# Start of a two-layer hybrid trunk: small first pieces of x, half of x's squares on GpSimd, warm-up products

## The reference

```
xn   = rms_norm(h, norm_g)                  # mean of squares over 2048
proj = xn @ w_in                            # 2048 x 5376
qa, fa, ia, ga, qb, kb, vb, gb, uc, gc = split(proj)
ya = rms_norm(hgrn2(qa, fa, ia))            # 4 heads of 128, gated linear recurrence
yb = window_attention(rope(norm(qb)), rope(norm(kb)), vb, sinks)   # 16 heads of 64, window 128
yc = pooled means (windows 2/4/8/16) minus the token, linear map, scale
h  = h + concat(ya*silu(ga), yb*silu(gb), yc*silu(gc)) @ w_out
```

## Time and profile before

| | us |
|---|---|
| median of three runs | 1633.53 |
| profiled execution: span from first to last instruction | 1632.0 |
| runs shown, above that span | 1.4 to 1.6 |
| PE busy | 1612.1 (99% of the span) |
| DVE busy | 915.2 (56%) |
| ACT busy | 645.5 (40%) |
| POOL busy | 20.8 (1%) |

### The profile page before, as it was taken

The page is one execution under the profiler, slowest core; times in us unless marked ns, Lnnn a source line. Parts: engine busy times, 40 slices in busy tenths (PEclk is TensorE's granted clock), DMA queues, the critical chain, the costliest instruction groups (busy, mean ns, idle before and its releaser), DMA issues.

```text
span 1632.0 us, 27854 instructions
## 1 busy us (share of the span) xinstructions
PE 1612.1 (99%) x11366; PEld 1493.0 (91%) x11366; DVE 915.2 (56%) x1897; ACT 645.5 (40%) x1280; POOL 20.8 (1%) x78
## 2 busy tenths in 40 slices
PE   6999999999999999999999999999999999999999
PEld 6999999999999999999998899889999988888887
DVE  7677877645666554434335678774555674443231
ACT  7676455423222432323237764553223233232121
POOL 0000000000000000000000000000000000000000
PEclk9999999999999999999999999999999999999999
DMA  6222210112121223344432221112111212234441
GB/s 251 79 104 78 79 53 29 51 53 78 57 74 62 94 80 115 124 138 135 140 118 79 103 78 66 39 52 78 53 68 63 79 52 103 104 121 137 145 147 48
DMA packets 28014, 147.23 MB, mean 90 GB/s; under 512 B 3568, under 2 KB 3696, under 8 KB 12656
## 3 DMA queue, kind: packets, MB, share of 16 engines
q1 hardware_dynamic: 27888, 145.46, 25.8%
HBM read 136.86 MB, written 8.52 MB: 89 GB/s over the span
## 4 chain that ended last, share of the span: by engine, by line
PE 96%; DVE 2%; issue 1%; ACT 0%; DMA 0%; SPq 0%; DVEq 0%
PE ps_gemm L816 80%; PE ps_mix L706 3%; PE ps_mix L742 3%; PE ps_mix L658 2%; PE ps_mix L672 2%; PE ps_mix L701 1%; PE ps_gemm L634 1%; DVE rstd L900 1%; PE ps_mix L786 1%; PE ps_mix L788 0%; PE ps_mix L718 0%; PE ps_mix L775 0%; PE ps_mix L737 0%; DVE w_lo L883 0%; DMA w_stage<-in_w_in 0%
## 5 line engine op out<-in xcount | busy, mean ns | idle before, releaser
L816 PE MATMUL ps_gemm<-x_hi,w_hi 128*128 128x264 f32 (+1 forms) x2304 | 561.7, 311 | 12.5 <-DVE w_lo L883 10.3
L816 PE MATMUL ps_gemm<-x_hi,w_lo 128*128 128x264 f32 (+1 forms) x2304 | 543.1, 304 | 0.0
L816 PE MATMUL ps_gemm<-x_lo,w_hi 128*128 128x264 f32 (+1 forms) x2304 | 542.6, 303 | 0.0
L816 PEld LDWEIGHTS ps_gemm<-x_hi,w_hi 128*128 128x128 f32 x2304 | 371.1, 189 | 32.9 <-DVE w_lo L883 11.1
L816 PEld LDWEIGHTS ps_gemm<-x_hi,w_lo 128*128 128x128 f32 x2304 | 370.8, 189 | 16.5
L816 PEld LDWEIGHTS ps_gemm<-x_lo,w_hi 128*128 128x128 f32 x2304 | 370.2, 189 | 14.4
L883 DVE TENSOR_TENSOR w_lo<-w_stage,w_hi 128x512 fp32r<-128x512 f32 x464 | 305.5, 689 | 104.0 <-ACT w_hi L440 92.7
L440 ACT ACTIVATE w_hi<-w_stage 128x512 fp32r<-128x512 f32 x464 | 265.3, 618 | 169.7 <-DVE z L960 122.7
L816 PE MATMUL ps_gemm<-mixed_hi,w_lo 128*128 128x264 f32 (+1 forms) x768 | 205.2, 322 | 0.0
L816 PE MATMUL ps_gemm<-mixed_lo,w_hi 128*128 128x264 f32 (+1 forms) x768 | 205.0, 321 | 0.0
L816 PE MATMUL ps_gemm<-mixed_hi,w_hi 128*128 128x264 f32 (+1 forms) x768 | 203.9, 320 | 0.0
(11 more groups left out here) (169 smaller groups left out, 1407.1 us busy)
## 6 DMA issues: line engine op xcount, KB each, us to landing
w_stage<-in_w_in SPq DMA_DIRECT2D x83, 1024.0 KB, 4.8
w_stage<-in_w_out SPq DMA_DIRECT2D x32, 1024.0 KB, 4.8
x_in<-in_xT SPq DMA_DIRECT2D x4, 1056.0 KB, 9.8
res<-in_xT SPq DMA_DIRECT2D x16, 264.0 KB, 3.0
h1T<-z SPq DMA_DIRECT2D x16, 264.0 KB, 3.4
res<-h1T SPq DMA_DIRECT2D x16, 264.0 KB, 3.0
out<-z SPq DMA_DIRECT2D x16, 256.0 KB, 3.2
rope<-in_c_rope SPq DMA_DIRECT2D x2, 528.0 KB, 3.6
```

The source lines that it names most:

```text
L816: ins = pe.matmul(g[:, bank, 0:size], ws[:, N % 2, tick], xs[:, k, c:c + size], start=tick == 0 and i == 0, stop=tick == TICKS - 1 and i == 2)
```

## The change

x comes in five pieces of 1, 3, 4, 4 and 4 tiles. prm and the first quarter of chunk 0's weights are issued from ScalarE's queue, not SP's. The squares of tiles 0 to 7 are made and added up by GpSimd into `vt`, as it gets the tiles (15 instructions, each waiting for the one before). Those of tiles 8 to 15 stay on ScalarE and VectorE, but leave the loop over k: they follow the weight quarters of chunk 1 at ticks 2, 5 and 8 (VectorE a tick later), four, two and two at a time. At tick 13 VectorE waits for GpSimd and adds `vt` to `rstd`. TensorE begins with three float32 matmuls of 512 columns on zeros, for which VectorE clears `z[:, 0]` whole.

```diff
+X_PIECES = ((0, 1), (1, 4), (4, 8), (8, 12), (12, 16))
+POOL_SQUARES = 8
+ACT_SQUARES = ((8, 9, 10, 11), (12, 13), (14, 15), ())
+SUMS_END = (KC - POOL_SQUARES + 1, 2 * KC - POOL_SQUARES + 1)
+WARM_MATMULS = 3
...
-            sp.dma_start(prm_sb[:], prm).then_inc(s_prm0, 16)
             load_x(0)
-            sp.dma_start(wst[:, 0, 0:4]..., w_in[0, 0, :, 0:4 * P]).then_inc(s_wfirst, 16)
             load_x(1)
+            load_x(2)
             sp.dma_start(wst[:, 0, 4:]..., w_in[0, 0, :, 4 * P:]).then_inc(s_w[0], 16)
-            load_x(2)
             load_x(3)
+            load_x(4)
             load_w(1)
...
                     sp.wait_ge(s_xlo, 16)
-                    sp.wait_ge(s_xsq, 16)
+                    sp.wait_ge(s_xsq, KC - POOL_SQUARES)
+                    sp.wait_ge(s_psq, 2 * POOL_SQUARES - 1)
...
+            for k in range(POOL_SQUARES):                       # GpSimd
+                for q, (k0, _) in enumerate(X_PIECES):
+                    if k == k0:
+                        pool.wait_ge(s_x[q], 16)
+                if k == 0:
+                    pool.tensor_tensor(vt[:], xin[:, 0], xin[:, 0], ALU.mult).then_inc(s_psq, 1)
+                else:
+                    pool.tensor_tensor(th[:], xin[:, k], xin[:, k], ALU.mult).then_inc(s_psq, 1)
+                    pool.wait_ge(s_psq, 2 * k)
+                    pool.tensor_tensor(vt[:], vt[:], th[:], ALU.add).then_inc(s_psq, 1)
+                    pool.wait_ge(s_psq, 2 * k + 1)
...
+            act.dma_start(prm_sb[:], prm).then_inc(s_prm0, 16)  # ScalarE
+            act.dma_start(wst[:, 0, 0:4]..., w_in[0, 0, :, 0:4 * P]).then_inc(s_wfirst, 16)
             act.wait_ge(s_prm0, 16)
...
                 x_high(0, k, xin[:, k])
-                if 1 <= k <= EARLY_SQUARES:
-                    x_square(0, k - 1, xin[:, k - 1])
...
-                    if N == 0 and tick == 12:
-                        for k in range(EARLY_SQUARES, KC):
+                    if N == 0 and tick in HI_TICKS:
+                        for k in ACT_SQUARES[HI_TICKS.index(tick)]:
                             x_square(0, k, xin[:, k])
...
+            pe.wait_ge(s_warm, 1)
+            for _ in range(WARM_MATMULS):
+                pe.matmul(M[:, 0], z[:, 0, 0:P], z[:, 0, 0:512], start=True, stop=True)
...
-            link(dve.memset(z[:, :, 0:PAD], 0.0))
+            link(dve.memset(z[:, 1, 0:PAD], 0.0))
+            dve.memset(z[:, 0, :], 0.0).then_inc(s_warm, 1)
...
-                if 1 <= k <= EARLY_SQUARES:
-                    x_sum(0, k - 1)
...
                     if N == 0 and tick == 13:
-                        for k in range(EARLY_SQUARES, KC):
-                            x_sum(0, k)
+                        dve.wait_ge(s_psq, 2 * POOL_SQUARES - 1)
+                        dve.wait_ge(s_ss, SUMS_END[0] - 1)
+                        dve.tensor_tensor(rstd[:], rstd[:], vt[:], ALU.add).then_inc(s_ss, 1)
...
                         w_low(N + 1, HI_TICKS.index(tick - 1))
+                        if N == 0:
+                            for k in ACT_SQUARES[HI_TICKS.index(tick - 1)]:
+                                x_sum(0, k)
```

More of the change, by code:

```diff
@@ L77, in mini_tick @@
     return RMS_TICK if MINI[n][0] == "rms" else MINI_TICK
-EARLY_SQUARES = 8
+X_PIECES = ((0, 1), (1, 4), (4, 8), (8, 12), (12, 16))
[3 more added lines that the diff above has]
+WARM_MATMULS = 3
 ROPE_CHUNKS = list(range(1, 10))
@@ L257, in build @@
         s_prm, s_prm0, s_rope = sem("const_in"), sem("prm_in"), sem("rope_in")
-        s_x = [sem(f"x_in{q}") for q in range(4)]
+        s_x = [sem(f"x_in{q}") for q in range(len(X_PIECES))]
+        s_warm, s_psq = sem("zeros_for_warm_up"), sem("pool_square_step")
         s_w = [sem("w_in0"), sem("w_in1")]
@@ L354, in load_x @@
             def load_x(q):
-                sp.dma_start(xin[:, 4 * q:4 * q + 4], xT[:, 4 * q:4 * q + 4]).then_inc(s_x[q], 16)
-            sp.dma_start(prm_sb[:], prm).then_inc(s_prm0, 16)
+                k0, k1 = X_PIECES[q]
+                sp.dma_start(xin[:, k0:k1], xT[:, k0:k1]).then_inc(s_x[q], 16)
             load_x(0)
-            sp.dma_start(wst[:, 0, 0:4].rearrange("p k c -> p (k c)"), w_in[0, 0, :, 0:4 * P]).then_inc(s_wfirst, 16)
             load_x(1)
+            load_x(2)
             sp.dma_start(wst[:, 0, 4:].rearrange("p k c -> p (k c)"), w_in[0, 0, :, 4 * P:]).then_inc(s_w[0], 16)
-            load_x(2)
             load_x(3)
+            load_x(4)
             load_w(1)
@@ L414, in _ @@
                     pool.wait_ge(s_xlo, 16)
-                    pool.wait_ge(s_xsq, 16)
+                    pool.wait_ge(s_xsq, KC - POOL_SQUARES)
                 pool.memset(vm[:], 0.0).then_inc(s_avz, 1)
@@ L448, in x_square @@
             def x_square(layer, k, src):
-                if 16 * layer + k >= 2:
-                    act.wait_ge(s_ss, 16 * layer + k - 1)
+                if layer:
+                    act.wait_ge(s_ss, SUMS_END[0] + k - 1)
+                elif k >= POOL_SQUARES + 2:
+                    act.wait_ge(s_ss, k - POOL_SQUARES - 1)
                 act.activation((ta_, tb_)[k % 2], src, ACT.Square).then_inc(s_xsq, 1)
+            act.dma_start(prm_sb[:], prm).then_inc(s_prm0, 16)
+            act.dma_start(wst[:, 0, 0:4].rearrange("p k c -> p (k c)"), w_in[0, 0, :, 0:4 * P]).then_inc(s_wfirst, 16)
             act.wait_ge(s_prm0, 16)
@@ L459, in _ @@
             for k in range(KC):
-                if k % 4 == 0:
-                    act.wait_ge(s_x[k // 4], 16)
+                for q, (k0, _) in enumerate(X_PIECES):
+                    if k == k0:
+                        act.wait_ge(s_x[q], 16)
                 x_high(0, k, xin[:, k])
-                if 1 <= k <= EARLY_SQUARES:
-                    x_square(0, k - 1, xin[:, k - 1])
                 if k % 4 == 0:
@@ L504, in _ @@
                         w_high(N + 1, HI_TICKS.index(tick))
-                    if N == 0 and tick == 12:
-                        for k in range(EARLY_SQUARES, KC):
+                    if N == 0 and tick in HI_TICKS:
+                        for k in ACT_SQUARES[HI_TICKS.index(tick)]:
                             x_square(0, k, xin[:, k])
                     if n == 1 and tick == RMS_TICK - 2:
-                        act.wait_ge(s_ss, 16 * layer + 16)
+                        act.wait_ge(s_ss, SUMS_END[layer])
                         act.activation(sqh[:], rstd[:], ACT.Copy).then_inc(s_sqh, 1)
@@ L894, in x_sum @@
                 sq = (ta_, tb_)[k % 2]
-                dve.wait_ge(s_xsq, 16 * layer + k + 1)
-                if k == 0:
+                first = 0 if layer else POOL_SQUARES
+                done = SUMS_END[0] if layer else 0
+                dve.wait_ge(s_xsq, layer * (KC - POOL_SQUARES) + k - first + 1)
+                if k == first:
                     dve.tensor_copy(rstd[:], sq).then_inc(s_ss, 1)
                 else:
-                    dve.wait_ge(s_ss, 16 * layer + k)
+                    dve.wait_ge(s_ss, done + k - first)
                     dve.tensor_tensor(rstd[:], rstd[:], sq, ALU.add).then_inc(s_ss, 1)
@@ L1204, in _ @@
                     if n == 1 and tick == RMS_TICK - 1:
-                        dve.wait_ge(s_ss, 16 * layer + 16)
+                        dve.wait_ge(s_ss, SUMS_END[layer])
                         square_low(norm_no(layer, n), sql[:], rstd[:], sqh[:])
```

## The result

The changed kernel takes 1641.4 us (median of 5 runs, 1641.25 to 1642.07), against 1633.53 for the kernel before: a ratio of 1.0048, 95% interval 1.0037 to 1.0059. It is 7.9 us slower. The profiled span is 1639.5 us, 7.5 above the 1632.0 of before.

The account below looks back on a forecast made before the run. PE bounds the kernel from 42 us, so only M's shift counts: first pieces and squares -3.2, turns with GpSimd +12.2, issues and warm-up 0, net +9.0, giving 1642.5 us; 8 in 10 range 1630 to 1651.

Parts of the forecast that it names:

- What bounds the kernel: From 42 us PE is busy; the whole change is a shift of M, the sum products, with N=2 4.32 us behind.
- Eight squares on GpSimd: Fifteen GpSimd instructions of 1.2 us take turns with VectorE's two-input ones before M: M +12.2 us.
- The 0.5 taken off for one-input instructions: On VectorE's chain before M: GpSimd reads beside semaphore gaps, copy, cast and first sum save 0.5 us in all.
- Rival 1: VectorE isn't held up by long GpSimd instructions: M 34.5, 3.2 us earlier, 1630.3 us; chance 0.22.
- rival 2: GpSimd keeps VectorE out for half its length only: M 39.4, 1.7 us later, 1635.2 us; chance 0.09.
- rival 3: GpSimd, over 1.7 us an instruction, is last by itself at vt's add: M 38.6, 1634.4 us; chance 0.04.
- First pieces: At the start, smaller x pieces bring the first product near 6.9, 2.3 us earlier; k=4 still waits for weights at 12.2.
- Two issues on ScalarE's queue: At the start, issues done by 1.7 us, before prm is used: 0 to +0.5 us on the first product, taken as 0.
- Squares out of the x loop: On VectorE in the x loop: x_lo ends at 22.2, 3.8 us earlier, chain behind 12.25; M 34.5, 3.2 earlier.
- Warm-up: Three products on zeros before PE's first product: at worst it comes 1.1 us late, k=4 has slack; taken as 0.
- a step of 0.12 from the start: Sign to look for in PE's first products: steps of 0.12 us, where 24 products had taken 0.22 each.
- Rival 4: Slow VectorE delivery drops PE to 0.22 a step; N=1 up to 2.8 us more, some 1 showing; within the 0.62 case.

Follow-up runs that it names:

- experiment 1: Changed kernel with GpSimd's fifteen instructions left out (squares of tiles 0 to 7 missing from the sum, add of vt replaced by an equal one): 1629.68 us.
- experiment 4: Changed kernel with four squares on GpSimd instead of eight, the other twelve late on ScalarE and VectorE: 1637.66 us.
- experiment 5: Changed kernel with no square on GpSimd, all sixteen made by ScalarE and added by VectorE behind the x loop: 1636.09 us.
- experiment 9: Whole computation, no GpSimd squares; unlike the kernel before, TensorE sums ScalarE's squares of tiles 0 to 7, sum product at tick 9, w's second quarter separate: 1629.66 us.
- experiment 2: Changed kernel with GpSimd's fifteen instructions turned into memsets of the same size, squares of tiles 0 to 7 not summed: 1629.4 us.
- experiment 7: Kernel before with the five x pieces only, all issues left on SP, w's first quarter ahead of the second x piece: 1634.66 us.
- experiment 6: Kernel before with only the five x pieces and the two issues on ScalarE's queue, squares and warm-up as before: 1634.1 us.
- experiment 8: Kernel before with only the three warm-up products on zeros added: 1634.5 us.

## Why the prediction was right

*What bounds the kernel.* Right. The change is a shift of the sum product M, and N=2 follows 4.3 us behind it: 4.31 after, 4.32 in experiment 1. It fails only where TensorE waits so long for M that its clock falls (6.1 in experiments 4 and 5), and where TensorE itself is the bound (4.8 in experiment 9).

*Eight squares on GpSimd*, the deciding step, forecast +12.2 on M. Measured +11.9, by leaving them out, with VectorE's step, GpSimd's rows and the end of the effect all as told. That the size came out so near is in part luck, because errors in it cancelled. An instruction takes 1.07, not 1.2, and a turn costs 0.93, not 1.1. Against that, I counted 2.8 us of idle VectorE between 7.4 and 12.9 (experiment 1 has 1.3 there), and let 3.5 of 15 turns fall into it and ahead of it for nothing, while 11.9/0.93 = 12.8 were paid, all but some 2. The 0.5 taken off for one-input instructions was not seen: GpSimd was done before those came. Rival 1 is refuted by the x_lo rows and experiment 1, rival 2 by the turn of 0.93 of 1.07, and rival 3 by GpSimd's end at 28.9, far ahead of the add of vt at 41.46.

The Trainium skill, SBUF - State Buffer (Who interferes with whom), has the order right: two inputs on VectorE against a reading GpSimd exclude each other, and a GpSimd that only writes does no harm (experiment 2 agrees, four x_lo in 2.81). Its "whole instruction" is slightly more than was measured, 0.93 of 1.07, and well above it for a copy, 0.365 of 0.63. For the price, the Trainium skill, GPSIMD Engine Reference (section 3.1), with 4497 ns for 2048 columns, gives an estimate of 1.2; the rows say 1.07.

*First pieces*: forecast was a first product at 6.9, and with all issues on SP it came at 7.11 (experiment 7). In the changed kernel it came at 10.20, through the two issues on ScalarE's queue (next step) and GpSimd's turns. k=1 to 3 were forecast for 7.4 (6.3 + 0.26 MB at 423 GB/s is 6.9) and landed at 6.8, as GpSimd's row at 6.81 shows; in experiment 7, with w's first quarter ahead of them on the queue, they landed at 9.3. The first product carried no weight in the sum, because k=4 was taken as the gate in any case. That held: without GpSimd's squares x_lo of k=4 to 15 run from where the weights' rest lands, and end at 21.5. It held only because the squares had left the loop; with them in it VectorE had no slack from k=1 on (experiments 6 and 7).

*Two issues on ScalarE's queue* failed as a step. They were put at nothing, with at most 0.5 on the first product. prm took 3.1 instead of 1.9, and w's first quarter 6.3 to 7.6 instead of 4.0, and it is the latter that the first product waits for: 8.93 in experiment 1, where 6.9 was forecast, and 10.16 against 7.11 in experiments 6 and 7. In the changed kernel GpSimd's turns add the 1.3 from 8.93 to 10.20. On M the price is hidden: 38.65 against 38.70.

*Squares out of the x loop*: forecast M = 34.5, measured 33.19 (experiment 1), 1.3 more gain than forecast. x_lo ended 0.7 before the forecast 22.2, because SP, with two issues fewer ahead of it, issued the weights' rest at 2.12 and not at 2.59, and w_hi of k=4 began at 11.54. The chain behind it took 33.19 - 21.5 = 11.7 instead of 12.25. This is the term by which the forecast of M, 46.7, stands above the measured 45.06, together with the 0.3 of the turns. No run moves the squares alone, without the pieces and the issues.

*Warm-up*: worth nothing, as said (experiment 8). The sign given for it, a step of 0.12 from the start, failed: the changed kernel's first twelve products go at 0.22, as before.

*Rival 4*, the clock: the fall came as described, its price didn't. The granted clock is 0.52 from 20 to 30 us:

```profile
core 0: us, PE busy (x) PEld busy (x) DVE busy (x) ACT busy (x) POOL busy (x), PEclk, DMA share, GB/s
...
20.00:30.00 10.00, 8.19 (x32) 6.84 (x33) 10.00 (x7) 1.96 (x4) 8.52 (x6) 0.52 0.11 43
30.00:40.00 10.00, 10.00 (x80) 9.87 (x80) 9.58 (x16) 5.15 (x9) 0.27 (x1) 0.97 0.29 107
```

TensorE, given a k each 1.6 us, fell to 1.2 GHz there. It still waited 1.42 us for M, so this cost nothing; some 1 us had been counted.

The forecast of 1642.5 was 1.1 above the 1641.4 measured. On M it was 1.6 high, and the medians lie 0.4 further apart than the spans.

## What to carry to other kernels

Work on GpSimd isn't beside VectorE when both read SBUF and VectorE's instructions have two inputs there: count GpSimd's length into VectorE's chain, turn by turn, and compare it with what the same work costs on VectorE. Here a square and its add cost VectorE 1.87 us in turns, and 0.83 as a late add (6.0 us and the 0.61 of vt's add, for eight). Before making a first transfer smaller or moving an issue to another queue, read which transfer the second step waits for: on a start that is bound by bytes the wait only moves. A sum over partitions is made by TensorE in any case, and it can take the adding too: two products of 0.12 us for each tile that ScalarE has squared, at the precision of fp32r.

## What was not expected of the hardware

A small transfer can lose its short landing: 49 KB landed after 1.9 us where it was issued 0.44 us ahead of x on the same queue, and after 3.1 us where it was issued on ScalarE's queue together with 0.26 MB of x on SP's. 256 KB of weights took 4.0 us on SP's queue (experiment 7) and 6.3 to 7.6 on ScalarE's, without a change in the program ahead of them. A wait of about 4 us in TensorE's products was followed by 1.2 GHz for the next 5.8 us (39.23 to 45.05), and waits of 1.4 to 2.0 at the same place were not. With the same three warm-up products and a gap of about 2 us, the first 24 products ran at 2.4 GHz in one execution (experiment 5) and fell to 1.2 GHz within them in two others (experiments 1 and 8), so such a warm-up isn't one to rely on.
